# Token tile by token tile on both sides of each norm in a three-layer transformer kernel

## The reference

```
x = layer_norm(ALPHA * x + mix(x) @ w_out, ln1_g, ln1_b)
h = square(relu(x @ ffn_w1))                                  # 4096 features
x = layer_norm(ALPHA * x + h @ ffn_w2, ln2_g, ln2_b)
x = x + sigmoid(x @ ple_w_gate) * rms_norm(p @ ple_w_proj)
```

## Time and profile before

| | us |
|---|---|
| median of 3 runs | 2552.9 (2551.55 to 2554.05) |
| profiled execution | 2554.0 |
| its span, first to last instruction | 2551.9 |
| busy in the span: PE, DVE, ACT | 2297.6 (90%), 1317.9 (52%), 1084.2 (42%) |
| mean granted TensorE clock | 0.948 |

### The profile page before, as it was taken

How to read it: one execution, slowest core, us unless ns; L and a number is a source line. 1 busy time by engine, 2 the same in 40 slices (tenths; PEclk the granted TensorE clock), 3 DMA queues, 4 the chain that set the end, 5 groups by cost and what they waited for, 6 DMA issues and landing times.

```text
span 2551.9 us, 30213 instructions
## 1 busy us (share of the span) xinstructions
PE 2297.6 (90%) x11002; PEld 1893.5 (74%) x11002; DVE 1317.9 (52%) x1895; ACT 1084.2 (42%) x1614; POOL 54.1 (2%) x70
## 2 busy tenths in 40 slices
PE   7957889999989998899999988889998849999994
PEld 5856667888867886678888867767877738888883
DVE  3456546333355334364333355642254458898896
ACT  2312525234223225444433423343324338888884
POOL 0000000000000000000000000000000000000001
PEclk8968999999999999999999989999998969999997
DMA  5301033223322220123233323202321249999995
GB/s 158 92 24 50 17 99 100 95 94 99 99 74 74 92 83 17 50 83 108 90 99 99 99 66 104 83 1 67 99 89 61 62 172 374 410 409 409 410 399 199
DMA packets 129129, 338.46 MB, mean 133 GB/s; under 512 B 10528, under 2 KB 11712, under 8 KB 129040
## 3 DMA queue, kind: packets, MB, share of 16 engines
q1 hardware_dynamic: 117744, 296.85, 33.0%
q0 software_dynamic: 7840, 27.59, 3.1%
q10 hardware_dynamic: 3456, 12.81, 1.2%
HBM read 320.96 MB, written 16.25 MB: 132 GB/s over the span
## 4 chain that ended last, share of the span: by engine, by line
PE 81%; DVE 11%; ACT 4%; issue 2%; DMA 2%; SPq 0%; POOL 0%; DVEq 0%; ACTq 0%; POOLq 0%
PE bank L1738 38%; PE bank L1741 17%; PE bank L2032 10%; PE bank L2069 5%; PE bank L1825 3%; PE bank L1805 2%; PE bank L1815 2%; PE bank L1760 1%; ACT arena L794 1%; PE bank L2012 1%; DVE xt_l L1116 1%; DVE X L1147 1%; DVE w_l L1098 1%; DVE X L1145 1%; DMA w_raw<-in_ev_w_in_dram 1%
## 5 line engine op out<-in xcount | busy, mean ns | idle before, releaser
L1098 DVE TENSOR_TENSOR w_l<-w_raw,w_h 128x1024 fp32r<-128x1024 f32 x370 | 448.4, 1223 | 763.5 <-ACT w_h L760 761.4
L760 ACT CAST w_h<-w_raw 128x1024 fp32r<-128x1024 f32 x370 | 386.4, 1052 | 902.8 <-PE bank L1738 660.6
L1738 PE MATMUL bank<-w_h,xt_h 128*128 128x512 f32 (+1 forms) x960 | 376.6, 392 | 21.5 <-DVE xt_l L1116 8.0
L1738 PE MATMUL bank<-w_l,xt_h 128*128 128x512 f32 (+1 forms) x960 | 374.7, 390 | 0.0
L1738 PE MATMUL bank<-w_h,xt_l 128*128 128x512 f32 (+1 forms) x960 | 374.4, 390 | 0.0
L1741 PE MATMUL bank<-xt_h,w_h 128*128 128x512 f32 x608 | 239.4, 394 | 13.2 <-DVE xt_l L1116 11.4
L1738 PE MATMUL bank<-w_h,ht_h 128*128 128x512 f32 x624 | 242.7, 389 | 0.0
L1738 PE MATMUL bank<-w_l,ht_h 128*128 128x512 f32 x624 | 242.7, 389 | 0.0
L1738 PE MATMUL bank<-w_h,ht_l 128*128 128x512 f32 x624 | 242.7, 389 | 0.0
L1098 DVE TENSOR_TENSOR w_l<-spare,w_h 128x1024 fp32r<-128x1024 f32 x184 | 220.5, 1220 | 41.2 <-ACT w_h L760 40.4
L1741 PE MATMUL bank<-xt_h,w_l 128*128 128x512 f32 x608 | 238.8, 393 | 0.0
(11 more groups left out here) (300 smaller groups left out, 3031.9 us busy)
## 6 DMA issues: line engine op xcount, KB each, us to landing
w_raw<-in_ffn_w_dram SPq DMA_DIRECT2D x128, 512.0 KB, 3.6
spare<-in_w_down_dram SPq DMA_DIRECT2D x92, 512.0 KB, 6.7
spare<-in_w_gate_dram SPq DMA_DIRECT2D x88, 512.0 KB, 7.2
w_raw<-in_w_up_dram SPq DMA_DIRECT2D x88, 512.0 KB, 6.4
w_raw<-in_w_in_dram SPq DMA_DIRECT2D x30, 512.0 KB, 3.7
w_raw<-in_ev_w_in_dram SPq DMA_DIRECT2D x28, 512.0 KB, 3.6
w_raw<-in_od_w_in_dram SPq DMA_DIRECT2D x24, 512.0 KB, 3.5
slot_y_dram<-slot_out ACTq DMA_DIRECT2D x23, 512.0 KB, 6.8
```

The costliest lines, as they stand in the source:

```text
L760: nc.scalar.copy(w_h[:, n % SLOTS, :], raw_of(n)).then_inc(sem("w_hi"), 1)
L1098: V.tensor_tensor(w_l[:, s_, :], raw_of(n), w_h[:, s_, :].bitcast(F32), ALU.subtract)\
L1738: mm = T.matmul(bank[set0 + m][:, 0:g.width], a[:, c, toks_of(m)], b[:, kk, :], start=first, stop=last)
```

## The change

Products ahead of a norm and behind it run with the token tile as outer loop (`tiles=True`): all four pieces for tile 0, then for tile 1, and so on. What lies between them is cut by token tile too: add, statistics, root, apply, eight transposes into two banks, two casts, two subtractions. On PE a tile's transposes are issued from inside the neighbouring product, behind the (tile, piece) that `then` names: tiles 0 and 1 in the last two tiles of the product ahead, tiles 2 and 3 in the first two of the product behind. On ACT and DVE the steps of the tiles and the splits of the coming weight pieces are listed in an order written out by hand. The FFN loop has three rounds, and the fourth is written out, its last product (`w2b`) by tiles. `proj0`, `proj1` use `out1`'s bank set. In the third block `mem` is normalised during the gates and transposed within `wo0`, and the cross products run `ck`, `cv`, `cq` instead of `cq`, `ck`, `cv`. The core of the diff:

```diff
-            def product(g, i=None, js=None):
+            def product(g, i=None, js=None, tiles=False, then=None):
...
+                for m, j in [(m, j) for m in ms_ for j in js] if tiles else [(m, j) for j in js for m in ms_]:
...
+                    if m == 0:
+                        pe.wait_ge(sem("w_lo"), at(n + 1, g.dn, i))
...
+                    if g.after in seam:
+                        chunk = g.chunk0 + g.kc * (j + 1) - 1
+                        if g.form == "feat":
+                            if m == j == 0:
+                                pe.wait_ge(sem("tr_lo"), tr.start[g.after] + 8)
+                        elif j == 0 or chunk // 4 != (chunk - g.kc) // 4:
+                            pe.wait_ge(sem("tr_lo"), tr.start[g.after] + 2 * m + chunk // 4 + 1)
...
+                    elif m == g.banks - 1:
                         mm.then_inc(sem("piece_used"), 1)
+                    if then and (m, j) in then:
+                        then[m, j]()
+            def transpose_tile(name, src_tile, i):
+                pe.wait_ge(sem("src_ready"), src.start[name] + i + 1)
...
+                for half in range(2):
+                    for c in range(4):
+                        mm = T.transpose(tile_bank(name, i, half)[:, toks_of(c)], src_tile(i, 4 * half + c), ident)
+                    mm.then_inc(sem("tr_done"), 1)
...
-                product(outp[1])
-                for g in proj:
-                    product(g)
+                product(outp[1], tiles=True, then={(2, 1): seam_tile(ln1, X, 0), (3, 1): seam_tile(ln1, X, 1)})
+                product(proj[0], then={(0, 0): seam_tile(ln1, X, 2)})
+                product(proj[1], then={(0, 0): seam_tile(ln1, X, 3)})
                 all_free(proj[1].g)
-                transpose(f"ln1_{layer}", tiles_of(X), waits=src_waits(f"ln1_{layer}"))
-                with pe.Fori(0, NQ) as i:
+                with pe.Fori(0, NQ - 1) as i:
                     for g in ffn:
                         product(g, i)
-                all_free(gate[0].g - 1)
-                transpose(f"ln2_{layer}", tiles_of(X), waits=src_waits(f"ln2_{layer}"))
-                for g in gate:
-                    product(g)
-                all_free(gate[1].g)
+                for g in ffn[:3]:
+                    product(g, NQ - 1)
+                product(ffn[3], NQ - 1, tiles=True, then={(2, 1): seam_tile(ln2, X, 0), (3, 1): seam_tile(ln2, X, 1)})
+                product(gate[0], tiles=True, then={(0, 2): seam_tile(ln2, X, 2), (1, 3): seam_tile(ln2, X, 3)})
+                product(gate[1], tiles=True, then={(2, 1): seam_tile(nxt, v, 0), (3, 1): seam_tile(nxt, v, 1)})
```

DVE's list in `tail` from the last round's `w2b` on (`split(n)` to `split(n + 3)` are `gate0`'s four pieces, `split(n - 1)` is the last one of `w2b`):

```diff
+                split(n - 1, None, 0)
+                dve.wait_ge(sem("gain_a"), gain_a[ln2])
+                for i in range(2):
+                    add_to_y(1, i, NQ - 1)
+                    tile_stats(ln2, last, i)
+                    tile_norm(ln2, i, 4)
+                add_to_y(1, 2, NQ - 1)
+                tile_stats(ln2, last, 2)
+                lo_tile(ln2, 0)
+                for j in range(3):
+                    split(n + j, None, 0)
+                tile_norm(ln2, 2, 4)
+                split(n + 3, None, 0)
+                lo_tile(ln2, 1)
+                add_to_y(1, 3, NQ - 1)
+                tile_stats(ln2, last, 3)
+                lo_tile(ln2, 2)
+                tile_norm(ln2, 3, 4)
```

ACT's list in `tail` at `gate1`; in layer 1 with the squares and roots of `m2`:

```diff
+                def last_sigmoid(i):
+                    sigmoid(1, i)
+                    if layer:
+                        square_tile("m2", X[:, i, :], i, (sem("x2"), i + 1))
+
+                last_sigmoid(0)
+                last_sigmoid(1)
+                hi_tile(nxt, 0)
+                sigmoid(1, 2)
+                split(n, None, 0)
+                if layer:
+                    square_tile("m2", X[:, 2, :], 2, (sem("x2"), 3))
+                split(n + 1, None, 0)
+                split(n + 2, None, 0)
+                hi_tile(nxt, 1)
+                split(n + 3, None, 0)
+                last_sigmoid(3)
+                hi_tile(nxt, 2)
+                hi_tile(nxt, 3)
```

More of the change, by code:

```diff
@@ L874, in tail, with ffn_up @@
[L874 to L885, removed]
+                def ffn_up(g, i):
+                    split_for(g, i)
+                    for m in range(4):
+                        h = 4 * (g.g - ffn[0].g) + m
+                        slot = TMP[:, m, :]
+                        act.wait_ge(sem("bank_full"), at(g.b + m + 1, g.db, i))
+                        if h >= 4:
+                            act.wait_ge(sem("hid_lo"), at(hid0 + h - 3, HID, i))
+                        own.do(nc.scalar.activation(slot, bank[g.set0 + m][:, :], ACT.Relu))
+                        own.do(nc.scalar.activation(slot, slot, ACT.Square))
+                        nc.scalar.copy(ht_h[:, h, :], slot).then_inc(sem("hid_hi"), 1)
@@ new lines, in tail @@
+                hi_tile(ln2, 3)
+                sigmoid(0, 1)
+                sigmoid(0, 2)
+                for j in range(4, 8):
+                    split(n + j, None, 0)
+                sigmoid(0, 3)
+                n = gate[1].n + 4
+                nxt = "m2" if layer else "x1"
+                def last_sigmoid(i):
[3 more added lines that the diff above has]
+                last_sigmoid(0)
@@ L973, in _ @@
                 split_for(g)
[L974 to L986, removed]
+            n = m2_sgu[1].n + LOOK
@@ L1932, in _ @@
             tail(1, tail1)
-            transpose("m2", tiles_of(XN), waits=src_waits("m2"))
-            for g in (m2_q, m2_kv, m2_su, m2_sv):
+            product(m2_q, tiles=True, then={(0, 1): seam_tile("m2", XN, 2), (1, 2): seam_tile("m2", XN, 3)})
+            for g in (m2_kv, m2_su, m2_sv):
                 product(g)
@@ new lines, in _ @@
+            product(m2_out[0], tiles=True, then={(0, 1): seam_tile("merged", GA, 3), (2, 3): memory_transposed})
+            pe.wait_ge(sem("tr_lo"), tr.start["mem"] + 4)
+            product(m2_out[1], tiles=True, then={(2, 1): seam_tile("cross", XN, 0), (3, 1): seam_tile("cross", XN, 1)})
+            product(c_k, then={(3, 0): seam_tile("cross", XN, 2), (3, 2): seam_tile("cross", XN, 3)})
+            pe.wait_ge(sem("tr_lo"), tr.start["cross"] + 6)
+            product(c_v)
+            product(c_q)
@@ L1971, in _ @@
+            all_free(c_q.g)
             attention("cross", cross_steps, c_probs, c_pt, c_ot)
-            for g in c_o:
-                product(g)
+            product(c_o[0])
+            product(c_o[1], tiles=True, then={(2, 1): seam_tile("moe", xn, 0), (3, 1): seam_tile("moe", xn, 1)})
+            transpose_tile("moe", tiles_of(xn), 2)
+            transpose_tile("moe", tiles_of(xn), 3)
             all_free(c_o[1].g)
-            transpose("moe", tiles_of(xn), waits=src_waits("moe"))
+            pe.wait_ge(sem("tr_lo"), tr.start["moe"] + 8)
```

638 lines of the change are left out of this document (436 added, 202 removed).

## The result

The changed kernel takes 2478.8 us (median of 4 runs, 2478.2 to 2480.0) against 2552.7 (2551.6 to 2554.1): 0.9711 of the time before, 95% interval 0.9694 to 0.9728, 73.9 us saved where 67 were forecast (2486, range 2465 to 2535). The profiled execution took 2478.2, its span 2476.4. The forecast held, and so did its reasons, but for one term of the sum that was sized wrong, at `m2`.

What follows compares the result with a forecast made beforehand. PE sets the time, standing in nine holes with slow starts behind them: 127.6 us before, 60.3 after, so 67.3 saved from 2554.0 gives 2486.7, or 2486 as median; range 2465 to 2535.

Steps and rivals of the forecast that it cites:

- one term of the sum: At `m2`: waits, transposes and a longer wait before `sv` cost 15.9 us against 15.4 before, so no gain.
- the nine holes: PE's standstills between products, one at each norm or merge: 121.0 us in all, all said to go.
- the slow starts: PE at lowered clock behind four of the long holes: 6.6 us in all, said to go too.
- `cross`: At the cross norm: transposes 3.5, `mem` 1.8 and a late `wo1` piece 0.9, 6.2 us against 19.6 + 1.2.
- Transposes and short waits: On PE at each place: 3.5 us for four tiles' transposes, plus waits from each engine's list, such as 5.5 at `ln2`.
- the rival of dear halves: Halves written by chunk take twice 0.68 and 0.63: 2516 us; chance 0.27 shared with late pieces.
- Late pieces: Each of 14 tile-ordered products waits for one more cast and subtraction: 2518 us, or 2540; chance 0.27 shared with dear halves.
- the falling clock: Short waits in the 14 tile-ordered products bring 1.2 GHz, 1.6 us each; four per product give 2576; chance 0.05.
- Covers hold: Rival: all places cost only transposes, `mem`'s 1.8 and 6.5 more at `moe`; saved 88, 2465 us; chance 0.06.
- 2 us or longer costs 1.6: Clock rule for PE: each new wait that long adds 1.6 us, shorter ones nothing; drawn from `sv`.
- What costs nothing: The written-out FFN round, `mem`'s norm during the gates, the earlier load of `m2`'s gain and SP's loads: no cost.

Runs made afterwards that it cites:

- e4: Changed kernel with the root of `m2`'s norm replaced on ACT by a square that needs no other table: 2474.4 us.
- e1: Changed kernel with `m2` alone put back: both products piece by piece, norm steps for all four tiles in turn: 2476.5 us, ratio 0.9715.
- e9: Changed kernel with 20 spare matmuls between `su` and `sv`, keeping PE at work while it otherwise waits: 2477.6 us.
- e6: Kernel before with only the fourth FFN round written out, matmuls in the old order: 2552.7 us against 2552.0, ratio 1.0002.
- e5: Changed kernel with `w2b` and `gate0` at `ln2` piece by piece again, transposes between them, other steps still cut by tile: 2506.5 us, ratio 0.9821.
- e7: Changed kernel with three orders mended: `m2_q` evacuation by tile, half statistics behind the last piece, order at `moe`: 2468.0 us, ratio 0.9679.

## Why the prediction was right, and where it was not

**What bounds.** Right: the nine holes and the slow starts were the whole of it. The six stretches around them hold all but 0.3 us of what was saved. Only `ln2` and `m2` were put back by runs; at `ln1`, `x1`, `merged`, `cross` and `moe` the stretches show what was saved, and not which part of the change saved it.

**Transposes and short waits.** Right within 1 us a place: four blocks of 0.87; 1.2 for the FFN's start (forecast 0.8), 0.3 for a fourth piece (0.8 and 0.5), 0.5 for tile 3's norm (1.0). The halves that write four chunks take what the row of the same element count takes: 681 ns on DVE and 590 on ACT for 72 of each (forecast 0.68 and 0.63). That rules out the rival of dear halves.

**Late pieces and the falling clock.** Both rivals are out. Beside the 1.4 in `m2_q` and the wait before `sv`, no piece comes more than 0.5 late (0.3 at `ln1` and `ln2`, 0.5 at `wo1`), and the granted clock is 1.00 in four of the six stretches. Covers hold nearly everywhere, at `moe` too; what keeps the time above that rival's 2465 is `m2`, at over 10 instead of 3.5, and the waits at `ln1` and `ln2`, some 1.5 to 2 a place.

**`m2`, the term that failed.** The prediction charged 15.9: waits of 2.8 and 3.7, 1.6 of half clock for each, 3.5 of transposes, 2.7 longer before `sv`. Measured: 1.4 and 1.6, none, 3.2, 2.7 (4.9 for 2.2, to the tenth), and 1.2 more of slow start behind the longer wait, which was not forecast: 10.1 (the stretch, less 5.1 for `ln2`, leaves 10.8). The two waits were too long because all seven loads were laid on ACT's path, while ACT in fact stands idle for DVE ahead of three squares of four (1.5 to 1.9). That the loads make these waits was right (e4). That the place gains nothing was wrong by 5: the tile order alone gains nothing there, but the hole of 15.4 held some 3.3 of waiting for a gain and 2 of uncut steps (e1). The clock was charged by a rule drawn from one wait, "2 us or longer costs 1.6", and neither wait reached 2.

**`cross`, and some luck.** 2.3 more was saved with `merged` than forecast. Of these 1.4 lie in the first 552 matmuls from the gates on, ahead of `merged`, where PE waits for nothing in either kernel: 128.3 before, 126.9 after, with the clock at 0.50 and 0.75 at their start (the windows under e9). Nothing in the prediction forecast that, and e9, with the same gates, has 128.3 again; it is luck. Another 0.4 is `wo1`'s fourth piece, 0.5 late instead of 0.9; the rest stays open.

**What costs nothing.** Right: the unrolled round (e6), the loads of SP (between 330 and 2000 us no cast waits for one), `mem`'s norm (PE is busy for 152.2 of the 152.2 us from the gates' start to behind `wo0`). The earlier load of `m2`'s gain stood in this list as a thing that could cost; by the traces it is a part of what was won.

## What to carry to other kernels

At a norm, ask how many us per tile the vector engine needs. Where a tile's norm is short, as at `m2`, cutting the steps by tile and loading the gain early won 5 of 15 with the matmuls as they were (e1), and the tile order no more; where it is long, the product ahead must finish its tiles early, and that order was worth 15 us of 21 at each `ln2` (e5). Look also at what a norm waits for besides the data: a gain that is loaded too late can hold the hole open. A product by tiles releases its weight slots and fills its last bank late, so look next at whoever is queued behind that last tile (here DVE before `sv`), and cut that work by tile too: e7 got 13 us from such orders, some 2 of them from the clock behind `sv`.

## What the runs showed of the hardware

A wait of PE of about 2.2 us is followed by a stretch at half clock in one run and not in another: in the kernel before, 96 matmuls behind a wait of 2.2 took 23.6; in e1 behind 2.20 they took 22.0 at a granted clock of 1.00:

```profile
1570.02:1592.03 22.01, 22.01 (x96) 17.91 (x96) 6.94 (x6) 4.94 (x6) 0.00 (x0) 1.00 0.54 166
```

Behind a wait of 4.9 the same 96 took 24.8 to 25.0 in four profiles and 23.45 in e5. That PE's standing still brings the clock down is shown (e9); what decides how far, for waits of the same length, is not. These phases move 1 to 3 us between `sv` and the gates from one profile to the next, as much as some edits, which is why the edits above are read by stretches.
